# Norms at three stage ends: GpSimd adds neighbouring squared tiles before TensorE's mean product

## The reference

```python
def rmsnorm(x, g):
    y = x * lax.rsqrt(jnp.mean(x * x, axis=-1, keepdims=True) + EPS)
    return y * g

for i in range(2):
    hn = rmsnorm(h, norm_mix[i])
    h = h + (conformer_conv(hn, ...) if i == 0 else ssd_mixer(hn, ...))
    h = h + swiglu(rmsnorm(h, norm_ffn[i]), ffn_w_gate[i], ffn_w_up[i], ffn_w_down[i])
y = rmsnorm(h, norm_final)
```

## Time and profile before

| what | value |
|---|---|
| median of 3 runs | 3510.59 us (3508.68 to 3511.5) |
| profiled execution | 3511.02 us |
| its span, first to last instruction | 3509.20 us |
| mean granted TensorE clock | 0.976 of full speed |
| TensorE matmuls | 3325.1 us busy, 95%, 19646 instructions |
| VectorE | 1591.2 us busy, 45% |
| ScalarE | 871.9 us busy, 25% |
| GpSimd | 937.8 us busy, 27%, 733 instructions |

### The profile page before, as it was taken

One profiled execution on the slowest core, in us unless ns is written; L12 is line 12 of the kernel. 1 busy time (PEld: TensorE's weight loads), 2 busy tenths in 40 slices (PEclk: granted clock), 3 DMA queues, 4 the chain that ended last, 5 costly groups with the idle time before them and its releaser, 6 DMA issues.

```text
span 3509.2 us, 52339 instructions
## 1 busy us (share of the span) xinstructions
PE 3325.1 (95%) x19646; PEld 3157.4 (90%) x19646; DVE 1591.2 (45%) x2619; ACT 871.9 (25%) x1569; POOL 937.8 (27%) x733
## 2 busy tenths in 40 slices
PE   4899969999999999697999999999989999999998
PEld 3888749999999999596998999999978999999997
DVE  3299952232222222545575575575654223222234
ACT  2111042211111111323333333433333111111113
POOL 2222122311211211233334333343333112112210
PEclk8999989999999999799999999999999999999999
DMA  3000001111111111010211211112111111111111
GB/s 98 25 29 26 18 5 37 49 42 42 42 48 42 42 42 53 18 40 25 63 50 36 62 40 40 56 30 62 44 38 31 42 42 42 47 42 42 43 47 58
DMA packets 226960, 147.25 MB, mean 42 GB/s; under 512 B 7784, under 2 KB 208840, under 8 KB 226854
## 3 DMA queue, kind: packets, MB, share of 16 engines
q1 hardware_dynamic: 226721, 145.96, 14.1%
q10 hardware_dynamic: 173, 0.39, 0.1%
HBM read 131.39 MB, written 15.65 MB: 42 GB/s over the span
## 4 chain that ended last, share of the span: by engine, by line
PE 84%; issue 6%; DVE 6%; ACT 2%; POOL 1%; DMA 1%; SPq 0%; DVEq 0%; POOLq 0%; ACTq 0%
PE bank L538 69%; PE bank L528 2%; PE bank L639 2%; PE bank L853 1%; PE bank L564 1%; PE bank L858 1%; PE bank L859 1%; PE bank L896 1%; PE bank L890 1%; DVE arena L1440 1%; DVE arena L1365 1%; DVE arena L1443 1%; DMA stage<-in_cf_w_pw 1%; PE bank L959 1%; DVE bank L1375 0%
## 5 line engine op out<-in xcount | busy, mean ns | idle before, releaser
L538 PE MATMUL bank<-xhi,whi 128*128 128x368 f32 x3840 | 1282.9, 334 | 32.5 <-POOL xlo L1811 25.3
L538 PE MATMUL bank<-xlo,whi 128*128 128x368 f32 x3840 | 1272.8, 331 | 0.0
L538 PE MATMUL bank<-xhi,wlo 128*128 128x368 f32 x3840 | 1270.0, 331 | 0.0
L1805 POOL TENSOR_TENSOR wlo<-stage,whi 128x1024 fp32r<-128x1024 f32 x220 | 546.7, 2485 | 1585.1 <-ACT whi L1001 1585.1
L538 PEld LDWEIGHTS bank<-xhi,whi 128*128 128x128 f32 x3840 | 725.5, 189 | 49.0 <-issue 31.4
L538 PEld LDWEIGHTS bank<-xlo,whi 128*128 128x128 f32 x3840 | 724.5, 189 | 3.5
L538 PEld LDWEIGHTS bank<-xhi,wlo 128*128 128x128 f32 x3840 | 724.9, 189 | 0.0
L1521 DVE TENSOR_TENSOR h<-h,bank 128x368 f32<-128x368 f32 x480 | 258.0, 537 | 684.1 <-PE bank L538 684.1
L538 PE MATMUL bank<-ahi,whi 128*128 128x368 f32 x1440 | 511.0, 355 | 0.3 <-issue 0.3
L538 PE MATMUL bank<-ahi,wlo 128*128 128x368 f32 x1440 | 477.1, 331 | 0.0
L538 PE MATMUL bank<-alo,whi 128*128 128x368 f32 x1440 | 477.1, 331 | 0.0
(11 more groups left out here) (211 smaller groups left out, 2985.8 us busy)
## 6 DMA issues: line engine op xcount, KB each, us to landing
stage<-in_ssd_w_in SPq DMA_DIRECT2D x48, 512.0 KB, 4.0
stage<-in_ffn_w_gate SPq DMA_DIRECT2D x44, 512.0 KB, 3.8
stage<-in_ffn_w_up SPq DMA_DIRECT2D x44, 512.0 KB, 3.8
stage<-in_ffn_w_down SPq DMA_DIRECT2D x44, 512.0 KB, 3.5
stage<-in_cf_w_pw SPq DMA_DIRECT2D x24, 512.0 KB, 4.0
arena<-in_state_ssm SPq DMA_DIRECT2D x16, 512.0 KB, 4.2
out_ss_s<-arena SPq DMA_DIRECT2D x16, 512.0 KB, 3.4
stage<-in_ssd_w_out SPq DMA_DIRECT2D x16, 512.0 KB, 3.5
```

Of the source, the lines that this page charges most:

```text
L538: mm = pe.matmul(bank[b][:, 0:TC], w[:, slot, w0:w0 + P], x[:, k, cs], start=n == 0, stop=n == 3 * len(offs) - 1)
L1805: pool.tensor_tensor(wlo[:, slot, :], stage[:, slot, :], whi[:, slot, :].bitcast(F32), ALU.subtract)\
```

## The change

A semaphore `n_pair` is added. At the three stage ends GpSimd adds the odd tile of a pair of squared tiles to the even one, in place (`norm_pairs`: 128x368 float32), and TensorE makes one mean product for the pair (`add_pair`). Chunks 0 and 1 are taken as four pairs each, chunk 2 as two pairs and four single tiles, so a norm has 14 mean products instead of 24. In TensorE's order the pairs 0 and 1 of a chunk stand behind products 4 and 6, pairs 2 and 3 behind products 0 and 2 of the next chunk. On ScalarE the root of chunk c-1 and its first hi copy stand one tile later; on VectorE the reciprocal and the scales do. On GpSimd four pairs of chunk 0 and two of chunk 1 stand ahead of everything; at S and F the other two pairs of chunk 1 stand behind the first xlo half, and the two of chunk 2 behind the second; at N the ten pairs are all there is, in a call that is new.

```diff
+        n_pair = sem("n_pair")
...
+            def add_pair(n, c, p):
+                q = n * NC + c
+                pe.wait_ge(n_pair, 10 * (n - N_SSD) + 4 * c + p + 1)
+                if p == 0:
+                    pe.wait_ge(n_x, 2 * q - 2)
+                mm = pe.matmul(bank[6 + q % 2][:, 0:TC], mean_w[:], work_of[n][c][:, 2 * p, :],
+                               start=p == 0, stop=p == 3)
+                if p == 3:
+                    mm.then_inc(n_sum, 1)
+
             def last_products(n, product):
 
                 for c in range(NC):
                     for k in range(KT):
                         product(c, k)
-                        if k >= 2:
-                            add_squares(n, c, [k - 2])
-                        elif c:
-                            add_squares(n, c - 1, [KT - 2 + k])
-                add_squares(n, NC - 1, [KT - 2, KT - 1])
+                        if k in (4, 6):
+                            add_pair(n, c, k // 2 - 2)
+                        elif c and k in (0, 2):
+                            add_pair(n, c - 1, 2 + k // 2)
+                add_squares(n, NC - 1, range(4, KT))
...
                     for k in ks:
                         square_tile(n, c, k)
-                        if c and not late and k == 0:
+                        if c and not late and k == 1:
                             root(c - 1)
-                        if c and not late and k == 4:
+                        if c and not late and k == 5:
                             hi(c - 1, 0)
                         if c and not late and k == KT - 1:
                             hi(c - 1, 1)
...
                         add(c, k)
-                        if c and k0 == 0 and k == 1:
+                        if c and k0 == 0 and k == 2:
                             invert(c - 1)
-                        elif c and k0 == 0 and 2 <= k <= 5:
-                            scale(c - 1, range(2 * k - 4, 2 * k - 2))
+                        elif c and k0 == 0 and 3 <= k <= 6:
+                            scale(c - 1, range(2 * k - 6, 2 * k - 4))
...
+            def norm_pairs(n, c, ps):
+                for p in ps:
+                    pool.wait_ge(n_sq, KT * (NC * n + c) + 2 * p + 2)
+                    w = work_of[n][c]
+                    pool.tensor_tensor(w[:, 2 * p, :], w[:, 2 * p, :], w[:, 2 * p + 1, :], ALU.add).then_inc(n_pair, 1)
+
             def norm_tail(n, u):
+                if n > N_FFN0:
+                    norm_pairs(n, 0, range(4))
+                    norm_pairs(n, 1, range(4) if n == N_FIN else range(2))
+                if n == N_FIN:
+                    norm_pairs(n, 2, range(2))
+                    return
                 for c in range(NC):
                     for half in range(2):
                         k4 = slice(4 * half, 4 * half + 4)
                         pool.wait_ge(n_hi, 2 * (n * NC + c) + half + 1)
                         pool.tensor_tensor(chunk(xlo, c)[:, k4, :], work_of[n][c][:, k4, :],
                                            chunk(xhi, c)[:, k4, :].bitcast(F32), ALU.subtract).then_inc(n_lo, 1)
+                        if n > N_FFN0 and c == 0:
+                            norm_pairs(n, 1 + half, range(2 * (1 - half), 4 - 2 * half))
                     if c == 0:
                         for j in range(2):
                             split(u + j, j)
...
             ffn(N_FFN1, U_FFN1)
+            norm_tail(N_FIN, None)
```

## The result

The changed kernel takes **3525.04 us** (median of five executions, 3523.64 to 3529.08), against 3510.59 before: ratio 1.0042, 95% interval 1.003 to 1.0054. Forecast were 3512.8 and no difference; it is slower by some 14 us. The profiled execution after took 3524.9 us, its span is 3523.1, its mean granted clock 0.970 (0.976 before).

A forecast was written before the change was run, and what follows sets the result against it. The prediction took the start of chunk 1's root at each stage end, not TensorE's total, to be the bound. 2.8 - 1.2 - 2.4 + 3.0 = +2.2 gave 3512.8 us against the median, range 3507 to 3518.

The forecast's parts named there:

- S: Stage end towards N_SSD: root of chunk 1 3.2 us later, one VectorE add fewer (-0.45), so +2.8 us.
- F: Stage end towards N_FFN1: root of chunk 1 at 2661.8, not 2662.67, less 0.45 for an add, so -1.2 us.
- N: Stage end towards N_FIN: no wait behind xlo, root of chunk 1 1.8 us earlier, in all -2.4 us.
- the clock: Behind TensorE's waits at S and F: lower clock costs 0 to 2.9 us each, taken as 1.5, +3.0 together.
- removed work: Three stages: each from 24 mean products to 14, 30 x 0.62 = 18.6 us of TensorE time saved.
- the sums' cost: On GpSimd: 30 added sums of 128x368, 0.98 us each.
- the wait of 5.0 us at S: Chunk 2 at S: TensorE waits 5.0 us for pair (1,2), which GpSimd sums behind the first xlo half.
- no cost on SP or in the splits: Weight splits follow the last root by the same distances, SP's weight loads move with them: costed at nothing.
- The rival without the wait: GpSimd has the pairs done before xlo, TensorE does not wait: S -1.5, F -5.0, total 3501.7; chance 0.08.
- The rival that hit the number: GpSimd sums cost 2.7 us each beside a working VectorE: +13.8, 3524.4 against the median; chance 0.07.

The follow-up runs named there:

- e7: Changed kernel with 24 added matmuls in TensorE's wait for pair (1,2) at S and F: 3520.37 us.
- e3: Kernel before with 17 added matmuls (2.9 us) ahead of the last product in front of group 0's chunk loop: 3520.09 us.
- e9: Kernel before with 7 added matmuls in each chunk of group 0's loop, 12 in the last two: 3518.96 us.
- e2: Changed kernel with pairs at N only, S and F as in the kernel before: 3507.54 us.
- e5: Changed kernel with GpSimd's late pair sums ahead of the xlo half they stood behind, at all stages: 3509.24 us.
- e6: Changed kernel with S as before the change, F and N paired, late pair sums ahead of the xlo half: 3504.72 us.
- e15: e5's kernel with one added float32 product of 512 columns in each chunk of group 0's loop, 9 in all: 3499.12 us.
- e4: Changed kernel with 4 added matmuls (0.67 us) ahead of the last product in front of group 0's chunk loop: 3518.41 us.
- e8: Kernel before with 6 added matmuls (1.0 us) ahead of the last product in front of group 0's chunk loop: 3524.53 us.
- e14: Changed kernel with one added float32 product of 512 columns in each chunk of group 0's loop, 9 in all: 3514.77 us.
- e16: e5's kernel with 4 added matmuls (0.67 us) ahead of the product in front of group 0's loop: 3506.23 us.
- e12: e8's kernel with group 0's loop filled by 7 added matmuls a chunk, 12 in the last two: 3537.32 us.

## Why the prediction was wrong

Its stage steps held; what failed is **the clock**. The step that failed most is one that is missing: the sum ends with the three stage ends, so what stands between them is put at nothing. The only word on it is that the weight loads behind the splits "move with it".

| term | predicted | measured |
|---|---|---|
| S with that wait filled | +2.8 | +3.0 (e7) |
| F with the wait behind xlo filled | -1.2 | +0.2 (e7) |
| N | -2.4 | -2.3 |
| clock behind that wait, S | +1.5 | +2.4 |
| clock behind that wait, F | +1.5 | +1.1 |
| clock at the products behind F | 0 | +1.5 |
| from S to group 0 | 0 | +0.9 |
| group 0's chunk loop | 0 | +8.8 |
| sum | +2.2 | +15.6 |

Less the 1.65 of the start-up that is 13.9, the difference of the two spans. F and N are known less well than the table looks. F costs -2.1 in the traces of e3 and e9, which leave it as it was: the fall of the clock within 2646 to 2647 has no counterpart there, and root 1 comes 2.1 us earlier. N with the same pairs costs -3.8 in e2, e5, e6, e7 and e15.

*Right:* removed work, the sums' cost, the wait of 5.0 us at S (4.62, and the restart within 0.1 us), N, no cost on SP or in the splits, and that the 18.6 us would be spent in waits (16.7 more of them ahead of mean products). The prediction's own figures for F, 2661.8 less 2662.67 and less 0.45, add up to -1.3, not -1.2. The rival without the wait was priced at S -1.5 and F -5.0; e5 and e6 measured -1.6 and -4.3 to -4.5.

*The clock term was mis-sized.* I bounded it by 0 and 2.9 at each stage and took 1.5 from the restart at 1449.15, where the clock was back after 3 us. Measured are 2.4 at S, near the upper bound, and 1.1 at F. The nearest row for S was the other one, 6.2 us from the restart at F, which follows an idle time behind a busy TensorE, as the new waits do. That the clock would fall once more at the products behind F, +1.5, had no term.

*F.* The sum for the mixer's norm of chunk 2 was to begin at 2636.5. It began at 2651.41, less the 13.4 by which F stands later: 2638.0. The first pair's wait, 2.92 us, brought the clock down (2645.65 above), where the wait of 2.82 at the same place had not. That is 1.5 us, and with it F's term. The length of the wait alone does not explain it: one of 2.83 in the kernel before and, at this place in e7, one of 2.34 were followed by the lower level too.

*From S to group 0.* The dt products start as far behind S as before, after 14.42 us of idle TensorE (14.41 before), but the chain gives them 14.39 us instead of 13.72: the clock is back 4.5 us after their start, not 3.0. The rest of the 0.9 was not followed.

*Group 0* had no term at all. I read the clock only where the change adds an idle time. The loop waits 1.48 us in each chunk and its clock stayed up in the trace of before, so I took it for a stage that shifts. e3, e4, e8 and e14 show that it doesn't: a few matmuls ahead of it take its clock down or bring it back, and so does S's delay; filling its waits does not keep the fall away, but brings the clock back in 7 us instead of 24. The Trainium skill, TensorE: Matmul & The Clock Gate, Part 1, which I weighed against the waits alone, has the lower clock as the default that activity releases; by that rule a loop that waits a third of its time is where to look too, and these traces agree.

*The rival that hit the number was wrong.* A costly sum on GpSimd was to give 3524.4; the sums took 969 ns, and S, F and N cost +5.9 together, not +13.8. Without the stage by stage reading the total would have confirmed it.

## What to carry to other kernels

A stage that the change only delays is not free: where TensorE waits in every turn, a microsecond of delay can cost 13 or give back 8 (e8, e16), so read the granted clock there before the change is blamed, and try the same kernel with a few matmuls more, whose results nobody reads. When a helper engine makes something for the bounding engine, put it ahead of the helper's longer work in its program: here two sums of 1 us moved ahead of 3.3 us were worth 7 us a stage. Filling a bounding engine's waits to hold its clock pays if it costs few instructions; 80 matmuls ahead of a loop cost 15 to 30 us in that loop, with the transfers of instructions doubled, and gave at most 14.

## What was not expected of the hardware

- The loop at the lower level: six matmuls (1.0 us) ahead of it made it 13.9 us longer, 1.0 and 12.9; one execution of the same program in eight was back at the old time.
- An idle time of 2.82 us left the clock up, and one of 2.92 and one of 2.34 (e7) in the same place brought it down; waits of 4.62 and 4.37 us cost 2.4 and 1.1 us more than they lasted, until the clock was back.
- The transfers of instructions went from 45 to 99 with 160 TensorE instructions more in one loop, and TensorE stood for some 3.4 us at a time in the loop behind it; 96 more instructions, at S and F in e7, left them at 44.
- The same code differs from execution to execution: the start-up by -2.4 to +3.6 us against the trace of before, F from -2.1 (e3, e9) to +1.7 (e12) with the F of before, and N with the end behind it from -1.2 to -3.8 with the same pairs at N. Single traces are to be compared stage by stage, medians for the total.
